# A hybrid encoder trunk in fp32: the order of the mixer's units, the convolution's form, the last merge and the start are changed

## The chip, the cores and the metric

One core of a Trainium2 chip runs the whole program, one launch for one inference step. The metric is device microseconds of that core, from the first instruction to the last; the median of three runs is used.

## The reference, cut to what matters

There are 640 tokens in all: 512 of one new stream and 8 running streams with 16 each. One layer is a half-step SwiGLU FFN, a mixer, and a second half-step FFN, each behind an RMSNorm.

```python
x = x + 0.5 * swiglu(rmsnorm(x))              # D_MODEL 1024, FFN 2816
P = rmsnorm(x) @ w_in                         # lru_x, lru_gate, z, xBC, dt, gate logits
xc = causal_conv(lru_x);  y_lru = gelu(lru_gate) * rg_lru_scan(xc)
xs, B, C = split(silu(causal_conv(xBC)))      # width 4; 2048 | 4 x 128 | 4 x 128
y = ssd_scan(xs, dt, A, B, C, h0) + D * xs    # 32 heads in 4 groups, state 128
y = rmsnorm_per_group(y * silu(z))
m = sigmoid(gA) * (y_lru @ w_br_lru) + sigmoid(gB) * (y @ w_br_ssd)
x = x + m @ w_out
x = x + 0.5 * swiglu(rmsnorm(x));  y_out = rmsnorm(x)
```

The convolution of a column tile is `y[t] = b + w0 x[t-3] + w1 x[t-2] + w2 x[t-1] + w3 x[t]`; for each stream it starts from that stream's three kept rows. Outputs are also the last three rows ahead of each convolution and the states of both scans.

## The kernel before, in words

**Layout and unit.** Activations lie with features on the 128 partitions and tokens in the free dimension (128 x 640 tiles). A *unit* makes one 128 x 640 output tile from 1024 inputs. Each fp32 operand is split into a high and a low part, and three products (high-high, low-high, high-low) are summed: 8 k-tiles x 3 x 2 halves of 320 columns, 48 matmuls (L588). Its result lies in one of two PSUM banks, `pu[o % 2]`; output o may start when VectorE has released output o-2, which lay in the same bank (`open_out`, L573). Two sides of weight buffers alternate: SP loads `w_raw`, ACT copies it into `w_hi` (L896), VectorE subtracts into `w_lo` (L1230). Both do this for unit u+2 in `take`, at the place in their queues where they are about to read unit u.

**Order of the program.** FFN1; dt; eight LRU pairs; then four mixer groups (`for g in range(GROUPS)`); two gate units gs6, gs7; the last merge; the output projection; FFN2; the final norm. The order is written out by hand, once for unit numbers (`mixer_order`, L51) and again in the queue of each engine: SP (L311 on), GpSimd (L403 on), TensorE (L571 on), ACT (L890 on), VectorE (L1221 on). An engine runs its queue in order.

**A group.** TensorE makes six xb units (four tiles of xs, then B and C). For each, ACT copies the result into `ext` behind three history columns (`to_ext`, L1000), VectorE convolves the 512 and the 8 x 16 columns apart (`convolve`, L1381 to L1395: two tensor_scalar, then six products, recorded at L1224), ACT takes tanh, VectorE makes the SiLU (one product). GpSimd writes the history of the sampled streams and saves the last rows (L443 to L457). Beside the second and third xb unit falls the norm of the group before (L1248 on). Then come four chunks of 128 tokens, t = 0 to 3: `scores` (transposes of xs at L745, B transposed, C times B, decay sums at L757 from the m_hi and m_lo that GpSimd builds at L529, ACT's exp into `lmat`, VectorE's products, the last of them lmat times cbm at L1574), the unit z(t), `inner` (L767, reads lmat and the decayed inputs), state products, and a branch unit with two outputs, br(g-1, t), whose two results VectorE scales and adds to `acc_ssd` (`branch_out`, L1511 to L1528). In group 0, which has no branch of a group before, the units bl(t) and gl(t+1) (LRU branch and LRU gate) stand there. The fifth chunk holds the sampled tokens: `scores`, two old outputs (16 transposes of the kept state, copied by VectorE into `h0_t`, L1612), a gate unit gs(2g-2), `inner`, two more old outputs, new states, and gs(2g-1). VectorE's multiplication by silu(z) (L1637), clearing (L1240) and adding (L1245) of the norm's sum stand between the old outputs' copies and the gate. ACT stores each gate's tanh by DMA.

**Last merge.** After gs6 and gs7 the norm of group 3 is summed and its branch units br(3, 0..3) run; per output VectorE scales, adds, multiplies by the gate, adds the LRU part, and makes the low part (L1679 to L1690), and ACT the high part. Then TensorE transposes the kept rows (L872), ACT copies them out of PSUM (L1199), and the output projection follows.

**Start.** SP loads the first unit's weights, then x; ACT issues 20 small parameter DMAs (L957 to L969) and cuts the first weights (L972); TensorE transposes x, VectorE copies it into `resid`, and ACT and VectorE split it into high and low parts, k-tile by k-tile.

These waits of TensorE set the path of a group:

```python
pe.wait_ge(s["xb_out"], g * 6 + 6)     # scores(0): all six tiles convolved
sv(t, SV_G)                            # inner(t): lmat * cbm done
pe.wait_ge(s["out_free"], o - 1)       # open_out(o): every unit, old and new output
```

## Time and profile before

| what | value |
|---|---|
| runs of the kernel before | 2061.96, 2059.88, 2058.93 us (median 2059.88) |
| the profiled execution's own time | 2059.99 us |
| its span in the trace | 2058.40 us |
| mean granted TensorE clock | 0.964 |
| TensorE matmul busy | 1913.9 us (93%) |
| TensorE weight load busy | 1856.7 us (90%) |
| VectorE busy | 1173.5 us (57%) |
| ACT busy | 599.5 us (29%) |
| GpSimd busy | 187.6 us (9%) |
| moved by DMA | 172.18 MB, 84 GB/s in the mean |

The span is the time from the first to the last recorded instruction; the profiled execution's own time is 1.59 us longer. Busy shares are of the span. In the rows PE is TensorE, PEld its weight loads, DVE VectorE, POOL GpSimd, SP SyncE; an entry in square brackets is idle time of that engine just before the instruction, and who ended it. PEclk is the TensorE clock that was granted, as a share of 2.4 GHz.

### The profile page before, as it was taken

Reading aid. Unit: us, or ns where it says so; the run is one execution under the profiler, and the core shown is the slowest. Engines: PE = TensorE matmul, PEld = TensorE weight load, DVE = VectorE, ACT = ScalarE, POOL = GpSimd, SP = SyncE. Lnnn points to the kernel's source line nnn. Section 1 sums busy time; section 2 is a strip of 40 time slices with the busy share of each in tenths; the row PEclk is TensorE's granted clock in tenths of the full one; section 3 lists DMA queues with packets and bytes.
Section 4 is the critical chain, followed back from the end, with each engine's and each line's share of the span. In section 5 each row is a group of like instructions: output and inputs, shape, how many; then the busy total and the mean of one; then the engine's idle time right before and its main releaser. Section 6 shows DMA issues by size and latency. Waiting matters only on the chain.

```text
span 2058.4 us, 31668 instructions
## 1 busy us (share of the span) xinstructions
PE 1913.9 (93%) x12827; PEld 1856.7 (90%) x12827; DVE 1173.5 (57%) x1524; ACT 599.5 (29%) x786; POOL 187.6 (9%) x273
## 2 busy tenths in 40 slices
PE   7999999997999799897997989798889999999997
PEld 7999999997999799797987888787789999999996
DVE  5442442445688755647668786787645442442444
ACT  4331221223576312132214123211333221221222
POOL 0000000000021211102212211220000000000000
PEclk9999999998999999998999999899989999999998
DMA  4222222223222323341233224123522222222222
GB/s 124 71 81 72 72 79 74 72 69 117 57 71 67 98 75 85 101 119 57 67 110 98 57 72 121 57 70 101 199 85 82 77 76 71 75 78 71 73 68 74
DMA packets 270349, 172.18 MB, mean 84 GB/s; under 512 B 8638, under 2 KB 261814, under 8 KB 269961
## 3 DMA queue, kind: packets, MB, share of 16 engines
q1 hardware_dynamic: 239792, 129.52, 22.1%
q0 software_dynamic: 6576, 26.26, 4.3%
q10 hardware_dynamic: 23900, 15.28, 2.4%
q8 instruction: 57, 0.93, 0.2%
q14 instruction: 24, 0.20, 0.0%
HBM read 150.54 MB, written 20.48 MB: 83 GB/s over the span
## 4 chain that ended last, share of the span: by engine, by line
PE 77%; DVE 13%; issue 5%; ACT 4%; ACTq 1%; DVEq 0%
PE pu L588 69%; DVE xf L1224 3%; ACT w_hi L896 2%; PE pn L818 1%; DVE w_lo L1230 1%; PE pn L767 1%; PE pn L783 1%; DVE lmat L1574 1%; PE pn L787 1%; DVE squares L1526 1%; PE pn L757 1%; DVE xf L1387 1%; DVE xc L1224 0%; PE pu L830 0%; DVE xf L1386 0%
## 5 line engine op out<-in xcount | busy, mean ns | idle before, releaser
L1230 DVE TENSOR_TENSOR w_lo<-w_raw,w_hi 128x1024 fp32r<-128x1024 f32 x241 | 295.2, 1225 | 654.3 <-ACT w_hi L896 652.4
L588 PE MATMUL pu<-act_hi,w_hi 128*128 128x320 f32 x2352 | 546.0, 314 | 23.2 <-DVE h_t L1612 10.3
L588 PE MATMUL pu<-act_lo,w_hi 128*128 128x320 f32 x2352 | 540.7, 311 | 2.1 <-DVE act_lo L1269 2.1
L588 PE MATMUL pu<-act_hi,w_lo 128*128 128x320 f32 x2352 | 540.0, 311 | 0.0
L896 ACT ACTIVATE w_hi<-w_raw 128x1024 fp32r<-128x1024 f32 x241 | 254.8, 1057 | 859.8 <-PE pu L588 857.5
L588 PEld LDWEIGHTS pu<-act_hi,w_hi 128*128 128x128 f32 x2352 | 398.8, 190 | 35.6 <-issue 27.4
L588 PEld LDWEIGHTS pu<-act_lo,w_hi 128*128 128x128 f32 x2352 | 396.9, 190 | 3.6 <-DVE act_lo L1269 3.1
L588 PEld LDWEIGHTS pu<-act_hi,w_lo 128*128 128x128 f32 x2352 | 397.5, 190 | 0.0
L588 PE MATMUL pu<-h_hi,w_hi 128*128 128x320 f32 x1056 | 241.0, 309 | 0.7 <-DVE ff_g L1286 0.7
L588 PE MATMUL pu<-h_hi,w_lo 128*128 128x320 f32 x1056 | 240.6, 309 | 0.0
L588 PE MATMUL pu<-h_lo,w_hi 128*128 128x320 f32 x1056 | 240.6, 309 | 0.0
L588 PEld LDWEIGHTS pu<-h_hi,w_hi 128*128 128x128 f32 x1056 | 176.5, 188 | 1.1 <-DVE ff_g L1286 0.9
L588 PEld LDWEIGHTS pu<-h_lo,w_hi 128*128 128x128 f32 x1056 | 176.6, 188 | 0.3 <-DVE h_lo L1295 0.3
L588 PEld LDWEIGHTS pu<-h_hi,w_lo 128*128 128x128 f32 x1056 | 176.6, 188 | 0.0
L1224 DVE SCALAR_TENSOR_TENSOR xf<-ext,vec,xf 128x512 f32<-128x512 f32 (+1 forms) x144 | 75.1, 586 | 0.0
L588 PE MATMUL pu<-yn_hi,w_hi 128*128 128x320 f32 x256 | 65.6, 338 | 9.9 <-DVE squares L1526 9.9
L1574 DVE TENSOR_TENSOR lmat<-lmat,cbm 128x1024 f32<-128x1024 f32 x20 | 58.7, 2934 | 3.2 <-ACT lmat L1136 3.2
L588 PEld LDWEIGHTS pu<-yn_hi,w_hi 128*128 128x128 f32 x256 | 44.8, 195 | 17.1 <-issue 9.3
L745 PE MATMUL pn<-ident,xf 128*128 128x128 f32 x80 | 14.0, 305 | 49.6 <-DVE xf L1224 49.6
L588 PE MATMUL pu<-yn_lo,w_hi 128*128 128x320 f32 x256 | 60.1, 317 | 0.0
L588 PE MATMUL pu<-yn_hi,w_lo 128*128 128x320 f32 x256 | 60.0, 316 | 0.0
L931 ACT ACTIVATE ff_t<-ff_g 128x640 f32<-128x640 f32 x44 | 32.5, 738 | 90.9 <-DVE ff_g L1286 90.9
(284 smaller groups left out, 1974.3 us busy)
## 6 DMA issues: line engine op xcount, KB each, us to landing
w_raw<-in_ffn_w_up_dram SPq DMA_DIRECT2D x88, 512.0 KB, 3.8
w_raw<-in_w_in_dram SPq DMA_DIRECT2D x73, 512.0 KB, 3.9
w_raw<-in_ffn_w_down_dram SPq DMA_DIRECT2D x32, 512.0 KB, 3.8
w_raw<-in_w_br_ssd_dram SPq DMA_DIRECT2D x16, 512.0 KB, 4.1
w_raw<-in_ffn_w_down_dram SPq DMA_DIRECT2D x16, 384.0 KB, 3.3
es<-e_spill POOLq DMA_DIRECT2D x40, 128.0 KB, 4.1
merged<-gate_spill POOLq DMA_DIRECT2D x8, 640.0 KB, 4.2
h_a<-in_state_ssd_h_dram POOLq DMA_DIRECT2D x8, 512.0 KB, 6.2
```

The lines of the kernel that those rows point to most:

```text
L588: ins = pe.matmul(dst[:, h, :], w[:, side, c, :], a[:, k, h * HALF:(h + 1) * HALF], start=(at == 0), stop=(at == n - 1))
L757: ins = pe.matmul(pn[1][:, b, :], gt_r[:, t // (NT - 1), :], m[:, 4 * b:4 * b + 4, :].rearrange("p h l -> p (h l)"), start=(part == 0), st ...
L767: ins = pe.matmul(pn[0][r:r + HD, 0, (h // 2) * P:(h // 2 + 1) * P], xd[:, h, :], lmat[:, h, :], start=True, stop=True)
L783: ins = pe.matmul(pn[0][:, 1, q * P:(q + 1) * P], ht[:, 2 * q:2 * q + 2, :].rearrange("n a b -> n (a b)"), xf[:, PAIRS + 1, t * P:(t + 1) ...
L787: pe.matmul(pn[1][:, 1, :], b_tok[:, :], xdd[:, :, :].rearrange("p h d -> p (h d)"), start=True, stop=True).then_inc(s["ssd_p"], 1)
L818: ins = pe.matmul(pn[0][:, 1, q * P + b * DEC_L:q * P + (b + 1) * DEC_L], h0_t[:, a, b, :], xf[:, PAIRS + 1, c:c + DEC_L], start=True, sto ...
L896: act.activation(w_hi[:, side, :, :], w_raw[:, side, :, :], ACT.Copy).then_inc(s["w_hi_done"], 1)
L931: act.activation(ff_t[:, :], ff_g[:, :], ACT.Tanh, scale=0.5).then_inc(s["ff_th"], 1)
L1224: return dve.scalar_tensor_tensor(out=dst, in0=a, scalar=scalar, in1=b, op0=op0, op1=op1)
L1230: dve.tensor_tensor(w_lo[:, side, :, :], w_raw[:, side, :, :], w_hi[:, side, :, :].bitcast(F32), ALU.subtract).then_inc(s["w_lo_done"], 1)
L1387: dve.tensor_scalar(ds, es_[:, :, 0:DEC_L], v(w), v(bias), ALU.mult, ALU.add).then_inc(s["conv"], 1)
L1574: done(dve.tensor_tensor(lmat[:, :, :], lmat[:, :, :], cbm[:, :].unsqueeze(1).to_broadcast([P, HPG, P]), ALU.mult))
```

## The change

- A table `FILL` gives the units of each group, and all queues read it. Units stand between the last xb unit and the first scores: z(g,0) and br(g-1,0) in groups 1 and 2, z and a bl unit in group 0, z alone in group 3. The xb units of B and C of the next group stand at the end of this group (group 0's ahead of the loop), so that four xb units are left at a group's head; B and C have buffers of their own (`bc`, one pair for even and one for odd groups). The gate units stand beside or right behind the fifth chunk's scores, ahead of the old outputs.
- The convolution treats the tile as 40 blocks of 16 columns. ACT writes `ext` as blocks of 19 (16 and three of history; two more small copies fill the history) and makes the first term with scale and bias; VectorE makes three products over all 640 columns.
- The second result of a br unit that stands ahead of scores is added behind the scores' products, so lmat comes ahead of it.
- All gates use one buffer `gbuf`, y_t lies in `es`. ACT's LRU stage waits for the product that reads xc before the next convolution.
- Last merge: the sum of the norm's squares stands ahead of gs7; rstd is multiplied into yn ahead of the split, so a branch result is only added to `acc_ssd`; ACT copies kept rows between its last high parts.
- Start: x is loaded first, the first unit's weights in four quarters, cut between the splits; the parameter DMAs are on SP's queue behind the second unit's weights; the sum of squares of x stands behind the first unit.

```diff
+FILL = {0: ([("z", 0, 0), ("bl", 0)],
+            [[("z", 0, 1)], [("z", 0, 2)], [("z", 0, 3)], [("gl", 4)]],
+            [[("gl", 1), ("bl", 1)], [("gl", 2), ("bl", 2)], [("gl", 3), ("bl", 3)], [("bl", 4), ("gl", 5)]],
+            [("bl", 5)], [("xb", 1, 4)], [("gl", 6), ("bl", 6), ("xb", 1, 5), ("gl", 7), ("bl", 7)]),
+        3: ([("z", 3, 0)],
+            [[("z", 3, 1)], [("z", 3, 2)], [("z", 3, 3)], [("br", 2, 3)]],
+            [[("br", 2, 0)], [("br", 2, 1)], [("br", 2, 2)], [("gs", 4)]],
+            [("gs", 5)], [], [])}
+for g in (1, 2):
+    FILL[g] = ([("z", g, 0), ("br", g - 1, 0)],
+               [[("z", g, 1)], [("z", g, 2)], [("z", g, 3)], [("gs", 2 * g - 2)]],
+               [[("br", g - 1, 1)], [("br", g - 1, 2)], [("br", g - 1, 3)], [("xb", g + 1, 4)]],
+               [("gs", 2 * g - 1)], [("xb", g + 1, 5)], [])
...
-            load(0, 0, 2, 0, cols(ffn1_w_up[0], 0))
             for t in range(NT):
                 src = x_prompt[0, t * P:(t + 1) * P, :] if t < NT - 1 else x_sample.rearrange("b l d -> (b l) d")
                 sp.dma_start(x_rows[:, t, :], src).then_inc(s[f"xin{t}"], 16)
+            for c in range(4):
+                sp.dma_start(w_raw[:, 0, 2 * c:2 * c + 2, :], cols(ffn1_w_up[0], 0, 2 * c, 2)).then_inc(
+                    s[f"w_part{c}" if c < 3 else "w_in0"], 16)
             load(1, 0, 2, 0, cols(ffn1_w_up[0], FFN))
...
+                sp.dma_start(vec_rows[r:r + src.shape[0], t, :], src).then_inc(s["params"], 16)
...
                         pool.wait_ge(s["ssd_p"], g * SP_GRP + SP * (t - 1) + SP_SEG)
+                    if t > 1:
+                        pool.wait_ge(s["ssd_v"], g * SV_GRP + SV * (t - 2) + SV_Y)
+                    if t > 0:
...
+                if g in (1, 2):
+                    xbc_front(g + 1, 4)
+                    xbc_last(g + 1, 4)
                 pool.wait_ge(s["ssd_p"], g * SP_GRP + SP * (NT - 1) + SP_SEG)
                 load_state(1)
                 pool.wait_ge(s["ssd_a"], g * SA * NT + SA * (NT - 1) + SA_BT)
...
+                if g == 0:
+                    xbc_front(1, 4)
+                    xbc_last(1, 4)
+                if g < GROUPS - 1:
+                    xbc_front(g + 1, 5)
+                    xbc_last(g + 1, 5)
...
+                    for w, a, name in ((w_hi, act_hi, "xh_done"), (w_lo, act_hi, None), (w_hi, act_lo, "xl_done")):
+                        if name:
+                            pe.wait_ge(s[name], XH_FFN1 + k + 1)
+                        for h in range(2):
+                            ins = pe.matmul(dst[:, h, :], w[:, 0, k, :], a[:, k, h * HALF:(h + 1) * HALF],
+                                            start=(k == 0 and a is act_hi and w is w_hi), stop=(k == KT - 1 and a is act_lo))
...
+                before, beside, behind, sampled_unit, middle, after = FILL[g]
+                for k in range(PAIRS):
                     mix_unit(("xb", g, k), act_hi, act_lo)
                     if g and k == 1:
                         norm_sum(SQ_GRP + g * SQG)
+                fill(before)
...
                 scores(NT - 1)
+                fill(sampled_unit)
                 old_states(0)
-                if g == 0:
-                    lru_branch_unit(4)
-                else:
-                    mix_unit(("gs", 2 * g - 2), act_hi, act_lo)
                 inner(NT - 1)
+                fill(middle)
                 from_states(0)
                 old_states(1)
                 pe.wait_ge(s["bseq"], g + 1)
                 new_states(0)
...
+            norm_sum(SQ_GRP + GROUPS * SQG)
             mix_unit(("gs", 7), act_hi, act_lo)
-            norm_sum(SQ_GRP + GROUPS * SQG)
...
+                act.wait_ge(s[f"w_part{c}" if c < 3 else "w_in0"], 16)
+                act.activation(w_hi[:, 0, 2 * c:2 * c + 2, :], w_raw[:, 0, 2 * c:2 * c + 2, :], ACT.Copy).then_inc(
+                    s["w_part_hi" if c < 3 else "w_hi_done"], 1)
...
+                if k % 2 == 0:
+                    cut_part(k // 2)
...
+            def to_ext(o, n, dst, w, bias):
+                pair = pu[o % 2][:, :, 0:HALF].rearrange("p h (b c) -> p h b c", c=DEC_L)
+                half = BLOCKS // 2
                 act.wait_ge(s["hist_in"], n + 2)
-                act.activation(ext[:, HIST:HIST + HALF], pu[o % 2][:, 0, 0:HALF], ACT.Copy).then_inc(s["ext_in"], 1)
-                act.activation(ext[:, HIST + HALF:EXT_P], pu[o % 2][:, 1, 0:SEQ - HALF], ACT.Copy).then_inc(s["ext_in"], 1)
-                act.activation(ext[:, EXT_P:EXT].rearrange("p (b c) -> p b c", b=DEC_B)[:, :, HIST:],
-                               sampled(pu[o % 2][:, 1, SEQ - HALF:HALF]), ACT.Copy).then_inc(s["ext_in"], 1)
+                act.activation(ext[:, :, HIST:BLOCK].rearrange("p (h b) c -> p h b c", h=2), pair, ACT.Copy).then_inc(s["ext_in"], 1)
+                act.activation(ext[:, 1:half + 1, 0:HIST], pair[:, 0, :, DEC_L - HIST:DEC_L], ACT.Copy).then_inc(s["ext_in"], 1)
+                act.activation(ext[:, half + 1:LAST + 1, 0:HIST], pair[:, 1, 0:LAST - half, DEC_L - HIST:DEC_L], ACT.Copy).then_inc(s["ext_in"], 1)
+                act.activation(halves(dst), pu[o % 2][:, :, 0:HALF], ACT.Identity, scale=v(w), bias=v(bias)).then_inc(s["ext_in"], 1)
...
+                    lv(LV_IX)
...
-                act.activation(halves(gs_buf[m % 2]), out(O_AT["gs", m]), ACT.Tanh, scale=0.5,
+                if m:
+                    act.wait_ge(s["gs_out"], 16 * m)
+                else:
+                    act.wait_ge(s["gl_out1"], 16 * 4)
+                act.activation(halves(gbuf[:, :]), out(O_AT["gs", m]), ACT.Tanh, scale=0.5,
                                bias=v(V_BG + KT + m)).then_inc(s["gs_th"], 1)
                 freed(("gs", m))
-                act.dma_start(gate_spill[m, :, TOK:2 * TOK], gs_buf[m % 2]).then_inc(s[f"gs_out{m % 2}"], 16)
...
+            def xbc(g, k):
+                name = ("xb", g, k)
+                n, c = XB_AT[name], xbc_tile(g, k)
+                take_mix(name)
+                if g and k < PAIRS:
+                    act.wait_ge(s["yn_lo_done"], (g - 1) * PAIRS + k + 1)
+                to_ext(O_AT[name], KT + n, xft(g, k), c + V_SCW + HIST * 24, c + V_SCB)
+                act.wait_ge(s["conv"], 2 * (KT + n + 1) + 1)
+                if g and k == 4:
+                    freed(("z", g - 1, 3))
+                elif n:
+                    act.wait_ge(s["xb_out"], n)
+                act.activation(rtmp[:, :], xft(g, k), ACT.Tanh).then_inc(s["xb_th"], 1)
...
                     act.activation(lmat[:, :, :].rearrange("p (b h) l -> p b (h l)", b=2), pn[1][:, :, :],
                                    ACT.Exp).then_inc(s["ssd_a"], 1)
+                    fill(held)
...
-                            take_mix(("br", g - 1, t), 1)
+                        fill(beside[t] + behind[t][:-1])
+                        held = behind[t][-1:]
...
             ssd_gate(6)
+            norm_rstd(GROUPS + 1, 0.25 / 512)
             ssd_gate(7)
-            norm_rstd(GROUPS + 1, 0.25 / 512, squares[:, 1, :])
+            for q in range(PAIRS):
+                act.wait_ge(s["xn_done"], KT + q + 1)
+                act.activation(yn_hi[:, q, :], squares[:, q % 2, :], ACT.Copy).then_inc(s["yn_hi_done"], 1)
...
+            for r in range(4):
+                branch(GROUPS - 1, r)
+                if r < 3:
+                    merged_split(2 * r)
+                    merged_split(2 * r + 1)
+            for a in range(TAIL_OUTS):
+                if a in (1, 3):
+                    merged_split(6 + a // 2)
+                tail_out(a)
...
+                if k % 2 == 0:
+                    c = k // 2
+                    dve.wait_ge(s["w_part_hi"] if c < 3 else s["w_hi_done"], c + 1 if c < 3 else 1)
+                    part = slice(2 * c, 2 * c + 2)
+                    dve.tensor_tensor(w_lo[:, 0, part, :], w_raw[:, 0, part, :], w_hi[:, 0, part, :].bitcast(F32),
+                                      ALU.subtract).then_inc(s["w_part_lo"] if c < 3 else s["w_lo_done"], 1)
...
+            def convolve(dst, n, per_o, i, o, w, step):
+                dve.wait_ge(s["ext_in"], n * 4 + 4)
+                blocks = dst.rearrange("p (b c) -> p b c", c=DEC_L)
+                for k in (2, 1, 0):
+                    ins = stt(blocks, ext[:, :, k:k + DEC_L], v(w + step * k), blocks, ALU.mult, ALU.add)
+                    if k == 2:
+                        ins.then_inc(s["out_free"], 1)
                         dve.wait_ge(s["out_free"], i * per_o + (o + 1))
                     else:
-                        dve.wait_ge(s["conv"], n * 7 + (2 * k - 1))
-                    stt(dp, ext[:, k:k + SEQ], v(w + step * k), dp, ALU.mult, ALU.add).then_inc(s["conv"], 1)
-                    dve.wait_ge(s["conv"], n * 7 + 2 * k)
-                    stt(ds, es_[:, :, k:k + DEC_L], v(w + step * k), ds, ALU.mult, ALU.add).then_inc(s["conv"], 1)
+                        ins.then_inc(s["conv"], 1)
+                    if k == 1:
+                        dve.wait_ge(s["conv"], n * 2 + 2)
...
+                else:
+                    dve.wait_ge(s["br_s"], n - KT + 1)
+                    dve.tensor_tensor(halves(acc), halves(acc), out(o), ALU.add).then_inc(s["out_free"], 1)
...
+            def xbc(g, k):
+                name = ("xb", g, k)
+                n, c = XB_AT[name], xbc_tile(g, k)
+                take_mix(name)
+                convolve(xft(g, k), KT + n, 0, 0, O_AT[name], c + V_SCW, 24)
+                dve.wait_ge(s["xb_th"], n + 1)
+                stt(xft(g, k), rtmp[:, :], 1.0, xft(g, k), ALU.add, ALU.mult).then_inc(s["xb_out"], 1)
...
+                held = before[1:]
+                fill(before[:1])
+                for name in held:
+                    begin(name)
                 for t in range(NT - 1):
                     scores(t)
-                    silu_z(g, t)
+                    for name in held:
+                        finish(name)
+                    fill(beside[t])
                     outputs(t)
-                    if g == 0:
-                        lru_branch(t)
-                        lru_gate(t + 1)
-                    else:
-                        for m in range(2):
-                            branch_out(g - 1, t, m)
+                    fill(behind[t][:-1])
+                    held = behind[t][-1:]
+                    begin(held[0])
...
+                finish(held[0])
                 sv(NT - 2, SV_Y)
                 for q in range(PAIRS):
                     dve.tensor_tensor(xf[:, q, 0:SEQ], xf[:, q, 0:SEQ], sz[:, q, 0:SEQ], ALU.mult).then_inc(s["yz"], 1)
                 clear_sum(g + 1)
                 for q in range(PAIRS):
                     add_square(SQ_GRP + g * SQG + q, q % 2, SEQ)
-                if g == 0:
-                    lru_branch(4)
-                else:
-                    ssd_gate(2 * g - 2)
+                fill(sampled_unit)
+                old_states(0)
+                decay_in(NT - 1)
+                decay_states(0)
+                fill(middle)
                 old_states(1)
...
             ssd_gate(6)
+            norm_scale(GROUPS + 1, 0.25 / 512)
+            dve.wait_ge(s["rs_step"], 4 * (GROUPS + 1) + 4)
             ssd_gate(7)
...
+            def split_last(q):
+                dve.wait_ge(s["yn_hi_done"], (GROUPS - 1) * PAIRS + q + 1)
+                dve.tensor_tensor(yn_lo[:, q, :], squares[:, q % 2, :], yn_hi[:, q, :].bitcast(F32),
+                                  ALU.subtract).then_inc(s["yn_lo_done"], 1)
+            for q in range(PAIRS):
+                if q >= 2:
+                    split_last(q - 2)
+                    dve.wait_ge(s["yn_lo_done"], (GROUPS - 1) * PAIRS + q - 1)
+                stt(squares[:, q % 2, :], xf[:, q, :], v(V_SNG + (GROUPS - 1) * PAIRS + q), rstd[:, :],
+                    ALU.mult, ALU.mult).then_inc(s["xn_done"], 1)
+            for q in (2, 3):
+                split_last(q)
```

Not shown: SP's, GpSimd's, ACT's and VectorE's queues follow the same table; semaphore counts follow.

## Rows read from the trace of the kernel before

The columns of rows 1 and 8 are: stretch, its length; busy us (instructions) of PE, PEld, DVE, ACT, POOL; PEclk; DMA share; GB/s. Rows of groups of instructions read: line, engine, operation, out<-in, partitions x elements, count | busy us, mean ns | idle time before, and who ended it.

**Rows 1.** Table by stretches, groups 0 to 3, last merge; the columns follow below.

```profile
667.00:901.60 234.60, 217.25 (x1473) 207.80 (x1472) 138.67 (x185) 53.94 (x79) 39.66 (x49) 0.96 0.34 92
901.60:1076.80 175.20, 156.88 (x1065) 147.52 (x1065) 128.69 (x176) 45.26 (x70) 37.22 (x45) 0.94 0.31 85
1076.80:1257.50 180.70, 157.54 (x1064) 147.06 (x1064) 139.41 (x184) 46.07 (x71) 35.85 (x44) 0.93 0.31 83
1257.50:1438.50 181.00, 157.65 (x1066) 147.21 (x1065) 139.55 (x184) 46.06 (x71) 33.94 (x40) 0.93 0.29 81
1438.50:1512.80 74.30, 55.90 (x335) 52.77 (x333) 50.03 (x63) 26.49 (x31) 4.83 (x9) 0.86 0.50 169
```

**Rows 2.** Chain that ended last: start us, us, engine, line.

```profile
23.96 14.38 PE pu L588 x96
...
731.13 14.08 PE pu L588 x96
...
1479.27 1.22 DVE w_lo L1230
...
1490.42 1.22 DVE w_lo L1230
```

**Rows 3.** Waits of TensorE: us in total, times, longest.

```profile
PE pn L745 <- DVE xf L1224: 49.6, 4, 12.9
...
PE pn L767 <- DVE lmat L1574: 9.4, 6, 1.6
```

**Rows 4.** Timeline, group 2: the norm's end, two convolutions, GpSimd's build.

```profile
1103.85 0.82 DVE L1224 SCALAR_TENSOR_TENSOR rstd<-squares,rstd 128x640 f32<-128x640 f32 x1
...
1118.80 0.55 DVE L1386 TENSOR_SCALAR xf<-ext,vec 128x512 f32<-128x512 f32 x1
...
1119.53 2.85 DVE L1224 SCALAR_TENSOR_TENSOR xf<-ext,vec,xf 128x512 f32<-128x512 f32 x6
...
1127.58 4.51 DVE L1224 SCALAR_TENSOR_TENSOR xf<-ext,vec,xf 128x512 f32<-128x512 f32 x6
...
1125.63 1.95 POOL L529 TENSOR_TENSOR m_hi<-da_hr,le_mask 128x1024 fp32r<-128x1024 f32 x1
```

**Rows 5.** Groups of instructions by line and form, group 2.

```profile
L896 ACT ACTIVATE w_hi<-w_raw 128x1024 fp32r<-128x1024 f32 x16 | 16.9, 1054 | 71.6 <-PE pu L588 71.6
...
L1224 DVE SCALAR_TENSOR_TENSOR xf<-ext,vec,xf 128x128 f32<-128x128 f32 x18 | 6.1, 339 | 0.0
...
L1224 DVE SCALAR_TENSOR_TENSOR xf<-rtmp,xf 128x640 f32<-128x640 f32 x6 | 5.0, 825 | 4.8 <-ACT rtmp L1128 4.8
...
L1005 ACT ACTIVATE ext<-pu 128x128 f32<-128x128 f32 x6 | 1.7, 285 | 0.0
```

**Rows 6.** Timeline, group 2: branch add, first lmat product, GpSimd's build.

```profile
1157.43 4.59 DVE L1528 TENSOR_TENSOR acc_ssd<-acc_ssd,squares 128x640 f32<-128x640 f32 x1
...
1138.33 5.36 DVE L1574 TENSOR_TENSOR lmat<-lmat,cbm 128x1024 f32<-128x1024 f32 x1 [0.84 <-ACT lmat L1136]
...
1138.83 1.91 POOL L529 TENSOR_TENSOR m_hi<-da_hr,le_mask 128x1024 fp32r<-128x1024 f32 x1
```

**Rows 7.** Timeline, end of group 3: VectorE, TensorE.

```profile
1408.07 2.48 DVE L1637 TENSOR_TENSOR xf<-xf,sz 128x512 f32<-128x512 f32 x4
...
1411.26 2.94 DVE L1245 TENSOR_TENSOR rvar<-rvar,squares 128x512 f32<-128x512 f32 x4
...
1404.89 0.87 PE L588 MATMUL pu<-act_hi,w_hi 128*128 128x320 f32 x2 [3.95 <-DVE h_t L1612]
```

**Rows 8.** Table by stretches: behind a hole, group 2.

```profile
1224.00:1230.00 6.00, 6.00 (x25) 6.00 (x26) 5.92 (x8) 1.24 (x2) 0.00 (x0) 0.55 0.14 42
```

**Rows 9.** Timeline, last merge: transposes of the kept rows.

```profile
1507.89 3.61 PE L872 MATMUL pn<-ident,tail 128*27 128x128 f32 x16 [8.51 <-ACT tail_rows L1199]
```

**Rows 10.** Timeline, start: ACT.

```profile
10.87 1.28 ACT L896 ACT_TABLE_LOAD   x1 [10.87 <-issue]
```

**Rows 11.** DMA view of the first 30 us, one figure for each 0.75 us.

```profile
GB/s 0 0 36 195 283 288 416 405 395 404 418 387 410 374 311 298 213 167 164 150 143 47 39 36 37 33 23 10 1 0 0 0 0 0 0 0 0 0 0 0
```

394 lines of the change are left out of this document (186 added, 208 removed).

## The prediction

> **What bounds the kernel now.** First the table by stretches [rows 1]: TensorE works in 157.5 of 180.7 us of group 2 and in 55.9 of the 74.3 us of the last merge. So its own work is the floor, and all that can be won is its idle time: 17.4, 18.3, 23.2 and 23.4 us in groups 0 to 3 and 18.4 at the merge. A unit (48 matmuls) steps by 7.04 us (96 matmuls in 14.08) in the chain that ended last [rows 2]. The waits name the holes [rows 3]: four times TensorE waits for the last convolution (49.6 us), six times for lmat (9.4). The timeline shows why [rows 4]: the sixth xb unit ends, and 12.9 us pass until the first transpose, because ACT's copy, VectorE's convolution, tanh and a last product follow one another, and this convolution's second part takes 4.51 us where its neighbour took 2.85, while GpSimd builds m_hi and m_lo. The other engines are idle in part, but at these places VectorE's queue is the path: it was busy 139.4 us of group 2.
>
> **Terms.** Durations: cutting weights 1.05 (ACT) [rows 5] then 1.22 (VectorE) [rows 2], a 640-wide product 0.83, the wait for a tanh 0.80 (4.8 us over 6) [rows 5]. I write X for the start of a group's first xb unit and E for the end of the unit ahead of the fifth chunk's scores.
>
> **1. One-piece convolution** (32 times). Two tensor_scalar and six products (3.58 us, from 1118.80 to 1119.53 + 2.85 [rows 4]) become three products of 640, 3 x 0.83 and two hand-overs: 2.6. ACT's three copies become four operations: two of 640, 0.72 each (between 1.05 for 1024 columns and 0.29 for 128 [rows 5]), and two small ones (0.29, half of it beside its neighbour): 1.7 in place of 0.8. The blocks of 16 columns at a pitch of 19 are nowhere at full width; the sampled part (8 such blocks) took 339 ns and the 640-wide product 825 [rows 5], 2.4 times for 5 times the columns, so I take full speed, and as the other bound half speed (1.66). A chain of a unit becomes 5.9 us instead of 6.5, both under 7.04: nothing on the path but 0.5 us where the chain is exposed. In the LRU stage it lies beside two units and the gates: nothing; if it were exposed, 8 x 0.5 either way. The added wait of ACT for the product that reads xc ends before ACT's square does: nothing.
>
> **2. Units between convolution and scores.** Convolutions of B and C leave this place, so the fourth xb unit is now the exposed one. In groups 1 and 2 the norm still falls on the second and third: its last product ended at 1104.67 [rows 4], 27.9 us after the group's first unit began (1076.8, the stretch's start [rows 1]); with a shorter convolution I take 27.3. Then cut 28.5, third convolution to 31.1, tanh 31.8; ACT cuts and copies for the fourth until 34.3; its three products with GpSimd's build beside them (m_hi and m_lo, 1.9 us each as the first of them [rows 4]) end at 39.3; tanh 40.1, product 40.9. TensorE ends the fourth xb unit at 29.1 (4 x 7.04 and 0.9 of norm sum), z at 36.4, the first half of br at 39.9. So the scores are covered by 14 us of work. But the second half of br needs the bank of z, freed after tanh(xb) 40.1, ACT's cut 41.1, tanh(z) 41.8, VectorE's cut 42.3 and the product: 43.1. New stall 3.2, and 0.3 ahead of z, whose bank the third convolution frees at 29.4. Group 3 has one unit only: it waits from 36.4 to 40.9, 4.5. Group 0 has no norm: none. Wait of 12.9 each becomes 3.5, 3.5, 4.8 and 0 (there 10.9 before, 49.6 less 3 x 12.9).
>
> **3. lmat ahead of the second branch add.** Before, the add was caught behind GpSimd (4.59 us for 0.82) and lmat came 1.56 us late [rows 3, 6]. Now lmat is caught in its place, as in the first chunk, where it took 5.36 us [rows 6] and ended 6.4 after the scores; that is ahead of inner (7.04): six times 1.56 gone, 9.4 us. What is late instead is the second half's release, scores + 8.3; the next br unit needs it at +10, except in chunk 3 of group 3, where br follows the scores directly and wants it at +3.5: stall 4.8. The weights cut there are wanted only after inner.
> In the first chunk lmat began 0.50 us before m_hi and still ended after m_lo, 3.8 us of builds later [rows 6]; GpSimd lost nothing. The Trainium skill, SBUF — State Buffer, section "SBUF: two separate sides", says that whichever of the two starts first holds the shared ports for its whole instruction. By it lmat would finish first and the sum would be up to 4 us lower; this trace disagrees, so the row decides.
>
> **4. End of a group.** Before: old states, then the gs unit 3.95 us late for h_t [rows 7]. After: scores, gs, old states; the second old output needs gs's bank. VectorE frees it behind: lmat (begins when ACT's exp ends at E+3.5, ends 4.7), cut 5.9, convolution of xb(g+1,4) 6.1 to 8.7, tanh 9.5, product 10.5 (b_seq on GpSimd costs 0.2), then sz products, clear and four adds with ACT's squares (together 6.1 us, as from 1408.07 to 1411.26 + 2.94 [rows 7]) to 16.6; ACT cuts for gs behind its last square (15.8 to 16.9), VectorE cuts 18.1 and adds: E+18.6. TensorE is there at E+10.4 (2.5 of scores, 7.04, one old): stall 8.2. Behind it VectorE copies old 1 only after the convolution of xb(g+1,5): 2.5; the next group's first output waits for a new-state add: 1.9; hp_rows 0.5. Sum 13.1 in groups 1 and 2. Without the convolution (group 3: gs, gs) the bank is free at 15.0: 4.6 + 1.9 + 0.5 = 7.0. Group 0 (gl5, bl5): 4.9 + 2.6 + 1.9 + 0.5 = 9.9.
> GpSimd's queue: load_state(1) now stands behind xbc_last(g+1,4), E+6.6, wanted at E+34; b_seq at E+9.6, wanted at E+38. load_decay's wait for an output two chunks back is long met. Stores keep their queue. All gates now share one buffer, so each tanh waits for the store before it; gs units lie 7 us or more apart and behind VectorE's lateness: nothing, and 2 us each for five of them as the upper bound.
>
> **5. Clock.** Behind a hole of 3.8 us the granted clock was 0.55, mostly the 1.2 GHz level [rows 8], worth up to 2.5 us. Groups 0 to 2 keep their number of such holes, group 3 has one more: -1.5.
>
> Groups: idle before less after: g0 17.4-9.9 = 7.5; g1 18.3-16.6 = 2 (rounded); g2 23.2-16.6 = 7 (rounded); g3 23.4-16.4-1.5 = 5.5. Sum 22.
>
> **6. Last merge.** The norm's sum goes ahead of gs7, rstd is folded into yn, the branch output needs one add. With T the end of gs6: rstd ready T+10.3 (ln, exp and two table loads as now), gs7's release 11.9 (its tanh waits for gs6's store, done by then), then eight 640-wide products and four copies: br can start at 13.6 and ends its first half at 19.0, where it was done at 11 before. So this costs a hole of 5.6. Then per unit VectorE took 11.15 us (1479.27 to 1490.42 [rows 2]), now two products less: 9.5. The first is 1 to 2 us longer, since ACT's cut waits for the slowed second half. VectorE's end comes at T+59 to 60 in place of 62.1. The larger part: the tail transposes stood behind it, an 8.5 us wait [rows 9]; ACT now takes four of five copies ahead of the last split, and the out projection starts at T+55.6 instead of 67.1. It reaches its last k at 61.8, behind VectorE. 11 us (bounds 3, if the projection waits for the last split, to 15).
>
> **7. Start.** ACT issued 20 DMAs and loaded a table until 12.16 before it cut anything [rows 10], and VectorE's resid copies stood behind that. Now x is first in SP's queue: 2.6 MB at about 400 GB/s from 3 us [rows 11] is in by 9.7; last transposes 10.7, copy 12.0. Then per k ACT 0.87, VectorE 0.95 (cuts of a quarter beside the split): first unit 13.2 to 21, the sum after it, second unit at 22.0 against 31.0 (23.96 and 7.04 [rows 2]). 9 us at full clock, 6.7 at the lower level: 8. 19 parameter DMAs now stand on SP's queue until about 13.5, ahead of the third unit's weights, which are wanted at 32; those weights also wait for the first cut.
>
> **Sum.** 22 + 11 + 8 = 41 us off the profiled execution's 2059.99 (span 2058.40, 1.6 around it, 0.1 above the median): 2019. Its own range, all terms at their bounds: 2006 to 2032.
>
> **Rivals.**
> A. VectorE is not late at the new places. Then the holes of 8.2, 3.2, 4.9, 4.8 and 4.6 with their clock, some 47 us, go too: 1972 in full, 1990 when half goes. For: it is idle 41 us a group. Against: every term of E+18.6 is a row. 14%.
> B. VectorE's queue gives back all in the groups, its lateness carried from one stage into the next: 8 + 11 only, 2041. For: group 1 gains 2 even in my sum. 13%.
> C. Slower: the 16-wide blocks run at half speed. Where: the three products of each xb unit. Chain 8.5 us over 7.04 for the 16 in rows, 2.6 each at 10 exposed ones: 16 x 1.5 + 26 = 50, time 2069. It decides from 1.6 us a product. Against: 339 ns. 4%. The Trainium skill, SBUF — State Buffer, section "Door 1", states that each access that crosses into a new 16-byte line pays; a block here touches five lines where four would do, an estimate of a quarter more, and 2025 in place of 2019. The sampled row shows no such price, so far as it is small and alone.
> That the change doesn't do what it says (xb units of B and C still ahead of the scores) the diff excludes.
>
> **Numbers.** My forecast 69%, A 14, B 13, C 4. The range 2003 to 2038 takes in my bounds, the near part of A and most of B. A measurement of this kernel tells about 0.2% (4 us) from no change. Faster 95%, within 1%, slower 4% (C).
>
> **What would show it.** Right: waits of the L745 transpose under 6 us in all; none for lmat in chunks 1 to 3; a new wait of 8 us of the second old output for the gs release, three times; 3 us inside the first br unit of groups 1 and 2; copies of tail rows before the last split; second unit at 22 us. Wrong: product on the blocks over 0.9 us, a hole ahead of units in the rows of xb, groups 1 and 2 far from 173.

## The result and the profile after

The changed kernel took 2044.78 us in the median of five runs (2038.52 to 2045.64) beside 2059.88 (2058.93 to 2063.38): ratio 0.9912, 95% interval 0.9892 to 0.9932. It is faster by 15 us where 41 were forecast, and outside the stated range. Run again beside the experiments it took 2039.30 (2038.00 to 2046.78; 0.9905, 0.9888 to 0.9922). The profiled execution took 2044.78 us, its span is 2043.2.

Two lines of the page show the busy time of the engines and TensorE's granted clock in 40 slices. Before, TensorE was busy 1913.9 us; the same number of products, 12827, now takes 16 us more.

```profile
PE 1930.1 (94%) x12827; PEld 1870.3 (92%) x12827; DVE 1154.3 (56%) x1363; ACT 627.2 (31%) x822; POOL 179.1 (9%) x241
...
PEclk8999999999999999899989997998899999999998
```

The table by stretches has the columns of [rows 1]: groups 0 to 3, then the stretch from the start of gs6 to the output projection.

```profile
668.56:909.67 241.11, 233.22 (x1587) 223.56 (x1588) 149.19 (x170) 68.92 (x100) 39.70 (x48) 0.97 0.34 94
909.67:1085.28 175.61, 160.69 (x1066) 149.18 (x1064) 128.06 (x143) 51.62 (x77) 33.62 (x36) 0.92 0.29 83
1085.28:1264.52 179.24, 163.43 (x1064) 151.74 (x1064) 135.37 (x155) 51.08 (x77) 35.31 (x40) 0.91 0.29 84
1264.52:1432.26 167.74, 150.45 (x968) 140.54 (x968) 125.89 (x145) 44.45 (x65) 32.59 (x32) 0.90 0.29 83
1432.26:1497.57 65.31, 53.62 (x333) 50.89 (x333) 43.54 (x55) 23.49 (x28) 4.85 (x9) 0.92 0.55 187
```

Group 0 now holds two units more and group 3 two fewer (14.1 us). (The first stretch of [rows 1] was cut 3 us late: group 0 ran from 663.93 to 901.57.) Like for like the groups changed by -10.6, +0.4, -1.5 and +0.9 us, so 10.9 us came out in all; the merge changed by -9.0 (65.3 for 74.3). The norm behind the first FFN shows what the start did: it came 4.7 us **later**. Its first products, before and after:

```profile
498.88 1.43 PE L603 MATMUL pn<-rvar,ones 128*128 128x320 f32 x2 [4.94 <-DVE rvar L1245]
```
```profile
503.62 1.43 PE L663 MATMUL pn<-rvar,ones 128*128 128x320 f32 x2 [4.94 <-DVE rvar L1320]
```

-10.9, -9.0 and +4.7 make the 15.2 us between the spans. The waits of TensorE after the change (us in total, times, longest), in which I call idle time inside a stretch a hole:

```profile
PE pu L891 <- DVE gbuf L1581: 23.7, 3, 9.5
PE pu L648 <- DVE sz L1299: 7.7, 2, 3.8
PE pn L713 <- DMA d_skip<-in_ssd_D_dram: 7.6, 1, 7.6
...
PE pu L648 <- ACT yn_hi L1253: 5.5, 1, 5.5
PE pn L830 <- DVE xf L1299: 5.3, 1, 5.3
...
PE pu L891 <- DVE gbuf L1575: 5.1, 1, 5.1
...
PE pu L648 <- DVE squares L1605: 4.8, 1, 4.8
PE pu L913 <- DVE h_t L1722: 4.5, 3, 1.9
```

All but the third were forecast: the second old output (L891) waits for the gate, br(g-1,0)'s second half for sz, the scores of group 3 (L830) for xs, br(2,3) for `squares`, the merge for yn_hi, the new states for h_t. The 49.6 us of [rows 3] are 5.3, its 9.4 us for lmat are gone. Idle time of the groups (length less busy) fell from 82.2 to 55.9 us, by 26.3, and yet only 10.9 came out: TensorE's busy time in them grew by 15.4. Two things were not in the forecast: the third wait, and this growth.

**The wait for d_skip.** SP's queue at the start and the DMA view from 20 to 34 us:

```profile
16.88 1.44 SPq L381 DMA_DIRECT2D d_skip<-in_ssd_D_dram  x2
21.20 13.43 SPq L341 DMA_DIRECT2D w_raw<-in_ffn_w_up_dram  x2
```
```profile
DMA packets 1500, 0.01 MB, mean 0 GB/s; under 512 B 1500, under 2 KB 1500, under 8 KB 1500
```

The two loads (2 x 4 KB) are 2048 packets of 4 bytes. They drain at 107 a microsecond (1500 in 14 us), and behind them in the queue stand the third and fourth unit's weights, whose two issues end 13.4 us after the first began. TensorE's history transposes wait until 40.1 us for the last of the 19 parameters. In the kernel before they drained about as slowly, on ACT's queue (1335 packets of it between 20 and 34 us), but TensorE waited for none of its parameters there.

**The clock.** Group 3's last products, in this profile and in that of the second run of the same kernel:

```profile
1407.87 1.97 PE L891 MATMUL pu<-ident,h_a 128*128 128x128 f32 x8 [4.78 <-DVE gbuf L1581]
1409.77 1.98 PE L852 MATMUL pn<-lmat,xd 128*64 128x128 f32 x16
1411.68 7.01 PE L901 MATMUL pn<-bc,h_t 128*128 128x16 f32 x32
...
1432.26 0.54 PE L648 MATMUL pu<-act_hi,w_hi 128*128 128x320 f32 x2 [2.04 <-DVE h_b L1739]
```
```profile
1407.36 1.74 PE L891 MATMUL pu<-ident,h_a 128*128 128x128 f32 x8 [4.79 <-DVE gbuf L1581]
...
1410.94 3.90 PE L901 MATMUL pn<-bc,h_t 128*128 128x16 f32 x32
...
1428.25 0.54 PE L648 MATMUL pu<-act_hi,w_hi 128*128 128x320 f32 x2 [0.68 <-DVE h_b L1739]
```

The hole ahead is the same 4.8 us. Then 32 products take 7.01 us in one execution and 3.90 in the other. The granted clock was 0.50 (1.2 GHz) from 1405.7 to 1422.8 in the first; in the second it rose in between. From the norm's sum of group 3 to that of the merge:

```profile
1279.24:1440.91 161.67, 144.38 (x921) 134.47 (x920) 118.21 (x136) 38.18 (x55) 29.54 (x26) 0.89 0.28 79
```
```profile
1280.90:1435.40 154.50, 138.33 (x922) 127.63 (x921) 118.24 (x136) 38.14 (x55) 29.21 (x26) 0.94 0.29 83
```

That is 7.2 us between two executions of one program, 6.1 of them busy time. From here on, "work at half clock" is TensorE's busy time while the clock was granted at 0.50, from the first xb unit of group 0 to gs6, and a "spell" is one piece of such time on end. It was 48.7 us before, 83.9 after and 77.0 in the second run. In the two rows above, 29.5 against 16.0 us of it cost 6.1 us, 0.45 for each. By that estimate the 35.2 us more of it in the groups are worth 16 us, and 15.4 were found.

Three experiments below (e1, e5, e4) leave the groups as they are, so with the two profiles above there are five executions of one and the same piece of program. Work at half clock and busy time there go together:

| groups 0 to 3, us | idle | busy | at half clock |
|---|---|---|---|
| before | 82.2 | 692.4 | 48.7 |
| after, run again (c1) | 55.1 | 704.7 | 77.0 |
| e1 | 54.8 | 706.6 | 81.1 |
| e5 | 55.9 | 707.8 | 83.7 |
| after | 55.9 | 707.8 | 83.9 |
| e4 | 53.7 | 712.9 | 94.6 |

From 77.0 to 94.6 us at half clock the busy time grows by 8.2 us, 0.47 for each, and the kernel before lies on the same line. So the growth is the clock's. The spread also says how large a difference in this number has to be before an edit can have made it.

### The profile page after: what moved, and what is told of

Its sections match the earlier page's. It is cut to its first block, busy times and chain, and to the rows that moved or that the text cites. A ratio compares the mean times of both kernels' runs of the same rounds, so it can differ in the third digit from the quotient of the medians.

```text
span 2043.2 us, 31544 instructions
## 1 busy us (share of the span) xinstructions
PE 1930.1 (94%) x12827; PEld 1870.3 (92%) x12827; DVE 1154.3 (56%) x1363; ACT 627.2 (31%) x822; POOL 179.1 (9%) x241
## 4 chain that ended last, share of the span: by engine, by line
PE 79%; DVE 10%; ACT 4%; issue 4%; DMA 2%; SPq 1%; DVEq 0%; ACTq 0%; POOL 0%; POOLq 0%
PE pu L648 71%; DVE xf L1299 2%; PE pn L852 1%; DMA d_skip<-in_ssd_D_dram 1%; PE pn L842 1%; ACT w_hi L969 1%; DVE bc L1299 1%; PE pn L870 1%; PE pn L901 1%; DVE w_lo L1305 1%; PE pn L874 1%; PE pu L913 1%; PE pu L891 1%; DVE squares L1299 1%; DMA merged<-gate_spill 0%
## 5 line engine op out<-in xcount | busy, mean ns | idle before, releaser
L648 PE MATMUL pu<-act_hi,w_hi 128*128 128x320 f32 x2336 | 543.7, 314 | 13.4 <-ACT act_hi L996 7.4
L648 PE MATMUL pu<-act_lo,w_hi 128*128 128x320 f32 x2336 | 535.3, 311 | 1.8 <-DVE act_lo L1344 1.5
L1671 DVE TENSOR_TENSOR lmat<-lmat,cbm 128x1024 f32<-128x1024 f32 x20 | 90.1, 4506 | 3.1 <-ACT lmat L1217 0.9
L1299 DVE SCALAR_TENSOR_TENSOR xf<-ext,vec,xf 128x640 f32<-128x640 f32 x48 | 54.6, 1137 | 6.7 <-ACT xf L1069 5.6
L1299 DVE SCALAR_TENSOR_TENSOR ff_a<-ff_t,ff_g 128x640 f32<-128x640 f32 x44 | 36.3, 825 | 35.4 <-ACT ff_t L1004 35.4
```

The source lines that it names most:

```text
L648: ins = pe.matmul(dst[:, h, :], w[:, side, c, :], a[:, k, h * HALF:(h + 1) * HALF], start=(at == 0), stop=(at == n - 1))
L1299: return dve.scalar_tensor_tensor(out=dst, in0=a, scalar=scalar, in1=b, op0=op0, op1=op1)
L1671: done(dve.tensor_tensor(lmat[:, :, :], lmat[:, :, :], cbm[:, :].unsqueeze(1).to_broadcast([P, HPG, P]), ALU.mult))
```

## The experiments

Each is an edit of the changed kernel, which stands at 2039 and 2045 us in its two sets of runs. Work at half clock is measured as above; five executions of the unedited groups had 77 to 95 us of it.

**c1_after_again**, nothing edited.

> The changed kernel itself, with nothing edited, beside the next three on the same chip. If its two clusters of times (2038.5 and 2045) come from spells of half clock in the rows of state products, its median lies between 2039 and 2046 with a spread of 5 us or more, and the profile shows the same holes to 0.1 us in the groups, while the length of its low spells in groups 0 to 2 differs from that of the first profile by 10 us or more. Rival (the clusters come from the late parameters at the start): the wait of the history transposes differs from 7.6 us by 5 us, the low spells do not.

2039.30 us (2038.00 to 2046.78). The larger holes of the groups agree to 0.1 us; the small ones ahead of new states and of the unit behind them differ by up to 1.4. The half-clock spells of groups 0 to 2 were nearly as long in sum (78 for 75 us), against my 10 us or more; the difference lay in group 3, where a spell of 17.1 us on end stood against three of 3.4. The wait for d_skip was 8.3 us, 0.7 more. So this pair differs by the clock and not by the start. The other executions point the same way: the granted clock was 0.964 in those of 2038 and 2039 us, and 0.957 in the one of 2046.78.

**e1_dskip_act**

The loads move to ACT's queue, behind g1_rows; the dots are the cut arguments.

```diff
-                    sp.dma_start(d_skip[...], ...).then_inc(s["params"], 16)
+                    act.dma_start(d_skip[...], ...).then_inc(s["params"], 16)
```

> The changed kernel with one edit: the two loads of d_skip are issued from ACT's queue, second and third in it, instead of last of the parameters on SP's queue. Theory (the two loads are 2048 packets of 4 bytes that drain at about 106 a microsecond; behind them SP's queue brings neither the parameters' last semaphore nor the third unit's weights): the 7.6 us wait of the history transposes goes, the third unit's weights land before 32 us, and with the low clock around the hole the time is 8 to 10 us under the changed kernel, about 2035. Rival (any small parameter behind 4.6 MB of x and weights on this queue is late, d_skip no more than the others): the hole shrinks by under 2 us, 2042 to 2045.

2040.67 us (0.9907, 0.9892 to 0.9922), between the changed kernel's two medians, where 2035 was expected. The wait at the history transposes went, and others came:

```profile
PE pu L727 <- DMA x_rows<-in_x_prompt_dram: 5.1, 2, 3.6
...
PE pu L643 <- DVE w_lo L1305: 2.1, 1, 2.1
```

The norm behind the first FFN began at 501.70 for 503.62. The theory of the queue holds and its price doesn't: beside the small packets x itself came later. The DMA view's GB/s in slices of 0.4 us, up to 16 us, first this kernel, then the changed one:

```profile
GB/s 0 0 0 0 37 124 197 266 338 369 359 440 389 389 389 400 185 92 92 246 215 215 185 185 226 236 206 206 117 136 105 130 128 102 94 64 49 45 50 53
```
```profile
GB/s 0 0 0 0 51 154 236 297 297 328 420 420 348 307 348 399 379 399 379 410 348 420 370 357 341 338 342 309 293 289 294 277 199 50 32 13 10 19 21 124
```

From 6.4 us on, SP's queue moves about 200 GB/s where it moved 380, while ACT's queue carries 0.01 MB in all.

**e5_dskip_late**

The loads move to GpSimd's queue, behind the spill of x, and have a semaphore of their own, for which VectorE waits ahead of group 0.

```diff
-                    sp.dma_start(d_skip[...], ...).then_inc(s["params"], 16)
+                    pool.dma_start(d_skip[...], ...).then_inc(s["dskip"], 16)
...
+            dve.wait_ge(s["dskip"], 32)
```

> The changed kernel with one edit: the two loads of d_skip are issued from GpSimd's queue at the end of the first FFN, where nothing waits for them before 742 us. Theory: no wait of the history transposes (7.6 us before), the third unit's weights in time, and no 13.7 us low spell at 37 us: 9 to 12 us under the changed kernel. Rival (with d_skip on ACT's queue nearly all was given back, as x came later; the load of x on SP's queue is the bound of the start whatever d_skip does): under 4 us.

2032.47 us (0.9863, 0.9846 to 0.9880), 7 to 12 under the changed kernel, where 9 to 12 were expected. There is no wait at the transposes, and SP issues the two weights in 3.1 us:

```profile
20.74 3.11 SPq L341 DMA_DIRECT2D w_raw<-in_ffn_w_up_dram  x2
```

The norm began at 492.48, 11.1 us ahead of the changed kernel's and 6.4 ahead of the kernel before: these 6.4 us are what the new start is worth without the small packets.

**e2_squares_behind** (VectorE; ACT's squares move behind its gate likewise)

```diff
                 finish(held[0])
+                fill(sampled_unit)
+                old_states(0)
+                decay_in(NT - 1)
+                decay_states(0)
                 sv(NT - 2, SV_Y)
...
                     add_square(SQ_GRP + g * SQG + q, q % 2, SEQ)
-                fill(sampled_unit)
-                old_states(0)
-                decay_in(NT - 1)
-                decay_states(0)
                 fill(middle)
```

> The changed kernel with VectorE's and ACT's order at the end of a group changed: the gate unit's add, the copies of the first old outputs and the first decay come ahead of the products with silu(z), the clearing and the four adds of squares. Theory (these 6.1 us of VectorE stand in front of the gate's add and hold its bank; and the 9.5 us holes they make cost a spell of half clock each besides): waits of the second old output 9.5, 9.5, 5.1 and 4.8 us become 3, 3, 0 to 1 and 0 to 2; a new hole of up to 3 us ahead of the first new states in group 3; low-clock work in groups down by 10 us; 12 to 20 us under the changed kernel, 2025 to 2033. Rival (VectorE's lateness is carried on and comes out at the copies of old outputs and new states): holes of 5 us reappear there, gain under 5 us, 2040 or more.

2026.03 us (0.9825, 0.9812 to 0.9838), 13 to 19 under the changed kernel. The rows that it moved stood in group 1 of the changed kernel like this, between the convolution's last product and the gate's add:

```profile
1046.02 2.49 DVE L1745 TENSOR_TENSOR xf<-xf,sz 128x512 f32<-128x512 f32 x4
1048.60 0.59 DVE L1315 MEMSET rvar<- 128x640 f32 x1
1049.22 2.94 DVE L1320 TENSOR_TENSOR rvar<-rvar,squares 128x512 f32<-128x512 f32 x4
...
1053.56 0.49 DVE L1581 TENSOR_SCALAR gbuf<-gbuf 128x640 f32<-128x640 f32 x1
```

The waits of the edited kernel:

```profile
PE pu L891 <- DVE gbuf L1582: 9.6, 3, 3.3
...
PE pu L913 <- DVE h_t L1723: 7.7, 4, 2.8
```

The holes came as expected, but for 2.4 us in group 0 and 3.1 in group 3, where up to 1 and 2 were said. Idle time of the groups fell from 55.9 to 40.4 us, and that is about what was gained. Work at half clock was 79.8 us, within the spread of the unedited groups, against "down by 10 us": a hole of 3.3 in place of 9.5 us did not bring the clock back.

**e3_unit_between** (in the unit order, TensorE's and VectorE's queue)

```diff
                 inner(NT - 1)
-                fill(middle)
                 from_states(0)
                 old_states(1)
+                fill(middle)
```

> The changed kernel with the unit xb(g+1,5) moved behind the second old outputs, so that in groups 1 and 2 a full unit stands between the small products on the kept states and the new states. Theory (TensorE's clock falls in a long row of small products and transposes, which the moved units used to break up; it was half for 20.5 us on end in group 2): low-clock work of groups 1 and 2 falls from 39 us to 25 or less and the time by 4 to 8 us with the holes as they are, 2037 to 2041. Rival (the 9.5 us hole ahead sets the clock, not what follows): low-clock work within 3 us of now and the time within 2 us, or later where the unit's bank is freed late.

2052.19 us (0.9959, 0.9947 to 0.9972), 7 to 13 slower. My theory falls, and the rival had it, with its "or later where the unit's bank is freed late": work at half clock of groups 1 and 2 was 44 us, where the changed kernel has 45 (the 39 of the expectation was too low), and the new states now wait for the bank of xb(g+1,5). Idle time of the groups rose by 4 us.

```profile
PE pu L913 <- DVE bc L1299: 7.9, 3, 2.6
```

**e6_end_order** (TensorE; VectorE copies the first old outputs behind `finish`)

```diff
-               [("gs", 2 * g - 1)], [("xb", g + 1, 5)], [])
+               [("gs", 2 * g - 1)], [], [("xb", g + 1, 5)])
...
+                old_states(0)
                 fill(sampled_unit)
-                old_states(0)
                 inner(NT - 1)
```

> The changed kernel with the end of a group ordered as in the kernel before: first old outputs straight behind the scores, then the gate unit, and xb(g+1,5) of groups 1 and 2 behind the new states; VectorE copies the old outputs ahead of the products with silu(z) and the squares. Theory (the gate unit covers VectorE's 6.1 us of squares, and the convolution of xb(g+1,5) no longer delays the copies that new states wait for; the small products then don't stretch, and the clock falls for single spells of 3.4 us only): the holes of 9.5 and 1.9 us become two of 3.5 and 2 us, low-clock work of groups 0 to 3 falls from 84 us to 55 or less, 15 to 22 us under the changed kernel. Rival (the low clock goes with the row of state products as such): holes fall as said and low-clock work stays over 70 us, 8 to 12 us under it.

2033.58 us (0.9867, 0.9852 to 0.9882), 6 to 11 under. In groups 1 and 2 there are two holes of 3.75 and 4.05 us, where 3.5 and 2 were said:

```profile
PE pu L648 <- DVE h_t L1722: 8.1, 2, 4.1
...
PE pu L891 <- DVE bc L1299: 7.5, 2, 3.8
```

Work at half clock is 67.6 us, clearly below the spread of the unedited groups, but not the 55 of my theory. The rival's figures, over 70 us and 8 to 12 under, lie nearest. Of what the groups gained, about 4 us are idle time and 4 to 7 are busy time, so the clock's.

**e7_both**: e5 and e6.

> Both edits, the late d_skip and the order at the end of a group. Theory: the two gains lie in different stretches and add up: 24 to 34 us under the changed kernel, 2010 to 2020. Rival (what is won at the start is given back by a start at a lower clock, or the end order's gain is clock alone): no more than the larger of the two.

2019.98 us (0.9799, 0.9786 to 0.9813), 19 to 25 under the changed kernel, at the near edge of what was expected. The parts (7 to 12 and 6 to 11) add. Work at half clock is 58.4 us, the least of all edits. Beside e5, from which only the order differs, all executions show a higher granted clock: 0.969 to 0.970 for 0.959 to 0.964.

**e4_merge_old**: the norm's sum stands behind gs7, `yn` is split from xf, and `rstd` multiplied into each result, as in the kernel before; the copies of kept rows stay between ACT's last high parts.

> The changed kernel with the arithmetic of the last merge as in the kernel before (rstd multiplied into each branch result, norm's sum behind the last gate unit, high and low parts of yn straight from xf), while ACT's copies of kept rows stay between its last high parts. Theory (both parts of the 9.1 us count: VectorE takes 11.2 instead of 9.5 us a unit but starts after a hole of 3.2 instead of 5.5): 3 to 5 us over the changed kernel. Rival A (all of it comes from the copies of kept rows): within 1 us of the changed kernel. Rival B (all of it comes from the shorter merge): 8 to 9 us over it, with an 8 us wait ahead of the kept rows' transposes or the projection.

2042.68 us (0.9908, 0.9894 to 0.9922). The time alone can't tell, since its runs (2038.40 to 2048.14) spread over more than the 3 to 5 us in question; the stretch can. From gs6 to the output projection it took 65.1 us where the changed kernel took 65.3 and 63.8, and its idle time there was 11.1 us beside 11.7 and 12.7 (18.4 in the kernel before). So rival A had it: the shorter merge is worth nothing that shows. The branch units now wait 9.9 us for results, and in the changed kernel 5.5 for yn_hi and 5.2 for results. The idle time won, 7 us, is left to the copies of kept rows, by elimination; no run took them away. The other 2 us of the 9 are busy time: work at half clock in the stretch fell from 14.8 to 9.0 us.

**e10_branch_first**: both halves of a br unit taken ahead of the next scores.

> The changed kernel with the order of the third part undone: both results of a branch unit are taken and added ahead of the next scores' products, lmat behind them (ACT cuts the weights there too). Theory (lmat is 1.6 us late six times as in the kernel before, and group 3's hole of 4.8 us at br(2,3) goes): 9.4 less 4.8, 3 to 6 us over the changed kernel's 2039 to 2045, so 2043 to 2050, waits of inner for lmat 8 to 10 us in all. Rival (the slow add beside GpSimd only changes places with lmat and costs nothing now that a unit stands behind each scores): waits of inner under 3 us, time within 3 us of the changed kernel or under it.

2048.06 us (0.9938, 0.9919 to 0.9957), 3 to 9 slower. The edited kernel waits for lmat again:

```profile
PE pn L852 <- DVE lmat L1677: 11.0, 7, 1.6
```

That is 11.0 us where 8 to 10 were said. The hole at br(2,3) is gone, as said. Part 3 was right in both signs.

**e8_late_squares**: e5 and e2. **e9_third_table**: e8 and

```diff
-            [[("z", 3, 1)], [("z", 3, 2)], [("z", 3, 3)], [("br", 2, 3)]],
-            [[("br", 2, 0)], [("br", 2, 1)], [("br", 2, 2)], [("gs", 4)]],
+            [[("z", 3, 1)], [("z", 3, 2)], [("z", 3, 3)], [("gs", 4)]],
+            [[("br", 2, 0)], [("br", 2, 1)], [("br", 2, 2)], [("br", 2, 3)]],
```

> The late d_skip together with the squares behind the first old outputs. Theory (they gained about 10 and 16 us apart, in different stretches): 2013 to 2018, under the end order's pair (2020). Rival (the parts share one clock budget and don't add): 2019 to 2025.

> As the last one, and in group 3 the unit br(2,3) and the gate unit gs4 change places, so that br(2,3) no longer stands directly behind the scores that hold br(2,2)'s second result. Theory (its 4.8 us hole is this bank, held by lmat's product and a weight cut): the hole of 4.8 us goes, none over 1 us takes its place, low-clock spell of 3.4 us with it: 4 to 6 us under the last one. Rival (VectorE's lateness is carried to the fifth chunk, whose old output then waits for br(2,3)'s second result instead of the gate): a hole of 3 us or more at the first old output of group 3, gain under 2 us.

e8 took 2018.56 us (0.9794, 0.9782 to 0.9807), half a microsecond above the theory's range and below the rival's. e9 took 2011.85 us (0.9764, 0.9751 to 0.9776), 6.7 under e8. The 4.8 us hole is gone and the second old output of group 3 waits 1.9 us; but 3.3 us stand ahead of its new states, where none over 1 was expected.

**e11_xb5_behind**: e9 with the first edit of e6, xb(g+1,5) behind the new states.

> As the group-3 table edit, and xb(g+1,5) of groups 1 and 2 stands behind the new states instead of ahead of the products on kept states. Theory (VectorE bound at the end of a group: its squares then delay the second old outputs' copies with no unit to cover them): the wait ahead of the first new states grows from 1 to 2 us to 4 to 5, low spells stay as long, 2 to 8 us slower than the group-3 table edit. Rival (it is the convolution of this unit that delays the copies): this wait goes to under 1 us, low spells of single 3.4 us, 3 to 8 us faster.

2005.96 us (0.9733, 0.9721 to 0.9746), the fastest, 54 us under the kernel before and 6 under e9. My theory had the sign wrong: the wait ahead of the new states fell from 2.1 us to nothing in group 1 and from 2.1 to 1.7 in group 2. So this unit's convolution did delay the copies in group 1, and hardly in group 2. The rival's single spells of 3.4 us did not come: in group 1 one spell lasted 17.1 us. The stretch from norm's sum to norm's sum there, where the kernel before took 175.2 us with 156.9 busy:

```profile
910.00:1082.40 172.40, 164.49 (x1065) 153.51 (x1065) 127.85 (x146) 50.18 (x76) 34.13 (x37) 0.91 0.30 84
```

## Why the prediction was wrong

**What bounds the kernel, terms, part 1: right.** A product on blocks of 16 took 885 ns in the LRU stage, where GpSimd has no builds, and the 640-wide row said 825:

```profile
L1299 DVE SCALAR_TENSOR_TENSOR xc<-ext,vec,xc 128x640 f32<-128x640 f32 x24 | 21.2, 885 | 5.2 <-ACT xc L1069 3.3 <-DVE xc L1299 1.1
```

Rival C and the estimate by the Trainium skill (SBUF — State Buffer, "Door 1", a quarter more, some 1030 ns) both fall; 7% more is what shows. Beside GpSimd's builds such a product took up to 2.4 us.

**Part 2: right.** The new waits were 3.8, 3.8 and 5.3 us where 3.5, 3.5 and 4.8 were said, and none in group 0.

**Part 3: right**, with its 4.8 us hole; e10 shows both. lmat is slowed beside GpSimd's builds in 16 of 20 chunks now, 4.5 us in the mean for 2.9 before. In each of the 16 it began 0.5 us ahead of m_hi and still took 5.3 us, against 1.2 alone, while the builds kept their 1.9. One of them:

```profile
1018.40 5.32 DVE L1671 TENSOR_TENSOR lmat<-lmat,cbm 128x1024 f32<-128x1024 f32 x1
```
```profile
1018.87 1.91 POOL L580 TENSOR_TENSOR m_hi<-da_hr,le_mask 128x1024 fp32r<-128x1024 f32 x1
1020.72 1.91 POOL L580 TENSOR_TENSOR m_lo<-da_lo,le_mask 128x1024 fp32r<-128x1024 f32 x1
```

The Trainium skill's rule (SBUF — State Buffer, "SBUF: two separate sides"), by which the one that starts first keeps the ports for its whole instruction, would have let it finish first, and is not borne out here either:

```profile
L1671 DVE TENSOR_TENSOR lmat<-lmat,cbm 128x1024 f32<-128x1024 f32 x20 | 90.1, 4506 | 3.1 <-ACT lmat L1217 0.9
```

**Part 4: right, up to 1.3 us a place.** The second old output waited 9.5, 9.5, 5.1 and 4.8 us for 8.2, 8.2, 4.9 and 4.6; the rest was less than said. Idle time in the groups is 55.9 us where 59.5 were forecast. (The groups' own sum, 22, is 21.3 before its terms are rounded.)

**Part 5, the clock: the step that failed first.** It said "Groups 0 to 2 keep their number of such holes, group 3 has one more: -1.5". Work at half clock rose by 35 us and took 15.4 of the 26.3 us of idle time won: a term of 1.5 measured 15.4. Counting holes was the wrong way to price it, since the holes shrank by a third in sum and work at half clock grew. The count did not see that the small products on kept states at the end of a group run slow for up to 20.5 us on end. Shortening the hole ahead did not end the spells (e2, e9), nor did putting a whole unit between these products (e3); only the end of a group in nearly its old order brought work at half clock below the spread of the unedited groups (67.6 us in e6, 58.4 in e7). What decides the length of a spell was not found, and executions of one program differ in it, from 77 to 95 us in sum; this cause stays open.

**Part 7, the start: the second.** "19 parameter DMAs now stand on SP's queue until about 13.5" took an issue for a landing: the last issue ended at 18.3 us, and the transposes could begin only at 40. The step gave the 19 loads no price by their packets. The start cost 4.7 us where 8 were to be won: 11.1 by the 2048 small packets (e5), and 1.6 because the start without them brings 6.4, not 8.

**Part 6: the sum near (9.0 for 11), its split wrong.** "VectorE's end comes at T+59 to 60 in place of 62.1" bought nothing that shows (e4). 7 us are left to "the larger part", the tail, and 2 are the clock's, which the sum had not in it.

The sum of 41 us fell short by 25.8: 12.7 at the start, 11.1 in the groups (13.9 by the clock beyond the 1.5 forecast, less 2.8 by which the idle time came out better than the sum had it), 2.0 at the merge. Rival B's figure (2041) lies beside the measured ones by luck. Its reason, VectorE's lateness carried on, is not the one: the holes were where and about as long as forecast.

## What to carry to other kernels

Idle time taken away is worth its length only if the granted clock stays as it was. Ahead of an edit, add up busy time at either level of the clock by stretch, and allow for losing part of the gain there: here 15.4 of 26.3 us went that way. Take the clock's own spread (here 77 to 95 us at half clock in one piece of program) from several profiles before a difference is laid to an edit. A load of single elements costs by its packets, not by its bytes, all that stands behind it in its queue and slows the neighbour's (2048 packets of 4 bytes cost 11 us here): put it where nobody waits. Before a release that another engine's next output needs, put nothing of the queue that can stand behind it (e2: 6 us of VectorE's work moved, 13 to 19 us won).

## What had not been expected of the hardware

- Packets of 4 bytes drained at 107 a microsecond on one queue, and the next two loads' issues took 13.4 us behind them (3.1 without). On a second queue they halved the first one's rate, from about 380 to 200 GB/s.
- Two executions of one program, with the same large holes to 0.1 us, differed by 7.2 us in a stretch of 160, 6.1 of them busy time under another granted clock.
- 32 products of 16 columns take 3.7 us at the full clock and 7.0 at half, so small products feel it nearly in full.
- A VectorE product that began 0.5 us ahead of a GpSimd build took 5.3 us, and 1.2 alone.
